# A routed expert layer on one core: token rows gathered by table products instead of through DRAM

## The reference

```python
comb = (p_grp[:, None, None] * grp_1h[:, :, None] * within[:, None, :]).astype(t.dtype)
out = jnp.zeros_like(t)
for gidx in range(N_GROUPS):
    e0 = gidx * EXPERTS_PER_GROUP
    e1 = e0 + EXPERTS_PER_GROUP
    a = jnp.einsum('td,edf->tef', t, w_exp_gate[e0:e1])
    u = jnp.einsum('td,edf->tef', t, w_exp_up[e0:e1])
    act = jax.nn.silu(a) * u * comb[:, gidx, :, None]
    out = out + jnp.einsum('tef,efd->td', act, w_exp_down[e0:e1])
```

## Time and profile before

| | |
|---|---|
| median of 3 runs | 769.56 us (767.94 to 770.43) |
| the profiled execution | 768.86 us, of which the span in the trace is 767.0 |
| PE busy | 713.2 us, 93% of the span |
| DMA moved | 187.25 MB, mean 244 GB/s |
| DVE, ACT, POOL busy | 274.3, 164.1, 61.1 us |
| granted clock of PE, mean | 0.974 |

### The profile page before, as it was taken

The page is one execution under the profiler, slowest core; times in us unless marked ns, Lnnn a source line. Parts: engine busy times, 40 slices in busy tenths (PEclk is TensorE's granted clock), DMA queues, the critical chain, the costliest instruction groups (busy, mean ns, idle before and its releaser), DMA issues.

```text
span 767.0 us, 10734 instructions
## 1 busy us (share of the span) xinstructions
PE 713.2 (93%) x4452; PEld 416.7 (54%) x4452; DVE 274.3 (36%) x733; ACT 164.1 (21%) x377; POOL 61.1 (8%) x91
## 2 busy tenths in 40 slices
PE   7999999999999999999999999999998977878974
PEld 3544557777656877777777775543333322323321
DVE  1241022575865651473264352151222101100335
ACT  3221221322455211321132102231000000000013
POOL 3010200010330000000010020020000000000110
PEclk9999999999999999999999999999999898999997
DMA  9983700770499521043144569487999999999991
GB/s 267 336 299 110 206 15 1 242 283 38 126 394 359 166 68 44 1 144 119 69 131 158 196 223 370 190 330 263 421 427 422 409 432 430 407 427 397 433 347 65
DMA packets 49465, 187.25 MB, mean 244 GB/s; under 512 B 5234, under 2 KB 5479, under 8 KB 45316
## 3 DMA queue, kind: packets, MB, share of 16 engines
q1 hardware_dynamic: 40064, 155.52, 52.4%
q0 software_dynamic: 9200, 30.80, 12.1%
q10 hardware_dynamic: 148, 0.20, 0.1%
HBM read 174.43 MB, written 16.83 MB: 249 GB/s over the span
## 4 chain that ended last, share of the span: by engine, by line
PE 76%; DMA 15%; DVE 4%; issue 2%; ACT 1%; SPq 1%; POOL 1%; DVEq 0%; ACTq 0%
PE PS L669 13%; PE PS L1017 13%; DMA arena<-in_w_exp_down 9%; PE PS L1434 8%; PE PS L1029 6%; PE PS L1468 6%; PE PS L764 5%; DMA ring<-in_w_exp_down 4%; DMA arena<-in_cache_mem_k 2%; PE PS L791 2%; PE PS L680 2%; PE PS L655 2%; PE PS L1316 2%; PE PS L750 1%; PE PS L1116 1%
## 5 line engine op out<-in xcount | busy, mean ns | idle before, releaser
L1434 PE MATMUL PS<-ring,arena 128*64 128x512 f32 x416 | 99.0, 632 | 13.6 <-issue 13.5
L1017 PE MATMUL PS<-hT,ring 128*128 128x288 f32 x384 | 102.2, 414 | 0.0
L1781 ACT ACTIVATE arena<-PS 128x512 f32<-128x512 f32 (+7 forms) x128 | 51.0, 421 | 181.5 <-PE PS L669 50.3
L1017 PEld LDWEIGHTS PS<-hT,ring 128*128 128x128 f32 x384 | 70.1, 190 | 19.6 <-issue 1.5
L1434 PEld LDWEIGHTS PS<-ring,arena 128*64 128x64 f32 x416 | 34.1, 145 | 73.5 <-issue 73.5
L669 PE MATMUL PS<-ring,hT 128*128 128x512 f32 x160 | 70.3, 596 | 0.0
L1781 ACT ACTIVATE brT<-PS 128x256 f32<-128x256 f32 (+4 forms) x37 | 15.6, 424 | 196.7 <-PE PS L1434 153.1
L764 PE MATMUL PS<-hT,ring 128*128 128x288 f32 x192 | 51.2, 422 | 1.3 <-DVE small L2347 1.3
L1029 PE MATMUL PS<-brT,ring 128*128 128x288 f32 x192 | 50.5, 412 | 0.3 <-DVE arena L2581 0.3
L669 PEld LDWEIGHTS PS<-ring,hT 128*128 128x128 f32 x160 | 29.9, 190 | 37.3 <-issue 37.3
L2993 DVE SCALAR_TENSOR_TENSOR brT<-brT,PS 128x256 f32<-128x256 f32 x16 | 6.7, 421 | 111.4 <-ACT brT L1781 111.4
(11 more groups left out here) (394 smaller groups left out, 851.7 us busy)
## 6 DMA issues: line engine op xcount, KB each, us to landing
ring<-in_w_in SPq DMA_DIRECT2D x15, 2048.0 KB, 13.8
ring<-in_w_exp_gate SPq DMA_DIRECT2D x13, 2048.0 KB, 23.9
ring<-in_w_exp_up SPq DMA_DIRECT2D x13, 2048.0 KB, 25.6
ring<-in_w_exp_down SPq DMA_DIRECT2D x8, 2048.0 KB, 24.5
arena<-in_w_exp_down SPq DMA_DIRECT2D x4, 2048.0 KB, 31.5
arena<-in_w_exp_gate SPq DMA_DIRECT2D x3, 2048.0 KB, 17.6
arena<-in_w_exp_up SPq DMA_DIRECT2D x3, 2048.0 KB, 22.5
moe_in<-in_table SPq DMA_DIRECT2D x2, 2048.0 KB, 24.4
```

What stands on the lines that cost most here:

```text
L1017: ins = pe.matmul(PS[:, b, 0:T], w[:, 512 * k + 128 * (c % 4):512 * k + 128 * (c % 4) + 128], hT[:, k, :], start=(k == 0), stop=(k == KD - 1))
L1434: ins = pe.matmul(o[64 * hf:64 * hf + 64, :], hg[:, k, 64 * e:64 * e + 64], w[:, :, 512 * k + 256 * hf:512 * k + 256 * hf + 256], start=(k ...
L1781: return act.activation(o, i, f, **kw)
```

## The change

The rows of all groups are now put into slots by one kind of product. `pick_slots` multiplies a 128-column piece of `h2p` (stationary) by the table of the pair (moving, 128 slots wide), summed over the three token tiles, so that the product comes out already turned, in the PSUM bank that the transposes wrote before. That is 24 matmuls for a pair, 8 pairs in all. The tables of group g+1 are made by DVE after the first expert of group g. `moe_in`, its zeroing, the scatter, the row reads, and ACT's copies of the picked rows are gone. `h2p` stays in place through the stage. Two small things move as well: `tails` gets another place, and `slots_out(1, p, 0)` on DVE stands behind the second expert.

```diff
-        def pick_rows(pr_):
+        def pick_slots(pr_, p, g):
 
-            pe.wait_ge(sg("h2p"), 3)
-            pe.wait_ge(sg("pick"), pr_ + 1)
+            if g == 0 and isinstance(p, int):
+                pe.wait_ge(sg("h2p"), 3)
+            pe.wait_ge(sg("pick"), 2 * G * p + (2 * g + pr_ + 1))
             for hf in range(2):
-                for t, (t0, n) in enumerate(TILES):
-                    ins = pe.matmul(bank_of(("pick", pr_, hf)), pick[pr_][0:n, t, :],
-                                    h2p[0:n, t, 512 * hf:512 * hf + 512], start=(t == 0), stop=(t == 2))
-                ins.then_inc(full[uses[("pick", pr_, hf)][0]], 1)
-
-        def turn_slots(pr_, p, g):
-
-            picked = g == 0 and isinstance(p, int)
-            if not picked:
-                pe.wait_ge(*((sg(f"xg{pr_}"), 16 * (3 * p + g)) if g else (sg(f"xf{pr_}"), 16 * p)))
-            for hf in range(2):
-                if picked:
-                    pe.wait_ge(*taken(("pick", pr_, hf)))
                 pe.wait_ge(*gtaken("xT", 2 * pr_ + hf, p, g))
                 o = gbank("xT", 2 * pr_ + hf)
                 for c in range(4):
-                    ins = pe.transpose(o[:, 128 * c:128 * c + 128],
-                                       xg[pr_][:, 512 * hf + 128 * c:512 * hf + 128 * c + 128], ident)
+                    for t, (t0, n) in enumerate(TILES):
+                        ins = pe.matmul(o[:, 128 * c:128 * c + 128],
+                                        h2p[0:n, t, 512 * hf + 128 * c:512 * hf + 128 * c + 128],
+                                        pick[g][pr_][0:n, t, :], start=(t == 0), stop=(t == 2))
                 ins.then_inc(gfull("xT", 2 * pr_ + hf), 1)
...
-            if g == 0 and isinstance(p, int):
-                pick_rows(0)
             if g == 0:
-                turn_slots(0, p, 0)
+                pick_slots(0, p, 0)
             for e in range(EG):
                 gate_up(e, p, g)
-                if e == 0 and g == 0 and isinstance(p, int):
-                    pick_rows(1)
                 if e == 1 and g == 0:
-                    turn_slots(1, p, 0)
-                if e == 1 and g < G - 1:
-                    turn_slots(0, p, g + 1)
+                    pick_slots(1, p, 0)
+                if e == 1:
+                    pick_slots(0, p, g + 1)
                 if e == 2:
                     turn_act(0, p, g)
                     turn_act(1, p, g)
-                if e == 3 and g < G - 1:
-                    turn_slots(1, p, g + 1)
+                if e == 3:
+                    pick_slots(1, p, g + 1)
...
-            if q == NPAIR - 1:
-                sp.wait_ge(sg("x_out"), 96 * (p + 1))
-                for pr_ in range(FIRST_PAIRS if first else 0, 2):
-                    sp.dma_start(xg[pr_], pair_rows(xrows, pr_, 0)).then_inc(sg(f"xf{pr_}"), 16)
...
-            if unit_no["gout"] <= n < unit_no["gout"] + 2:
-                r = 512 * (n - unit_no["gout"])
-                sp.dma_start(xrows[r:r + 512, :].rearrange("(p c) n -> p c n", p=128), bc(zrow, 128, 4, D)) \
-                    .then_inc(sg("zeroed"), 16)
...
+        def pick_tables(g):
+
+            for pr_ in range(2):
+                e = EG * g + 2 * pr_
+                tt(pick[g][pr_].rearrange("p t (e j) -> p t e j", e=2),
+                   bc(cst[:, C_IOTA:C_IOTA + SLOTS].unsqueeze(1).unsqueeze(1), 128, 3, 2, SLOTS),
+                   bc(rkm[:, :, e:e + 2].unsqueeze(3), 128, 3, 2, SLOTS), ALU.is_equal) \
+                    .then_inc(sg("pick"), 1)
...
-                if e == 0 and g == 0:
+                if e == 0 and g < G - 1:
+                    if g == 0 and isinstance(p, int):
+                        dve.wait_ge(sg("tail_out"), 32)
+                    pick_tables(g + 1)
+                if e == 1 and g == 0:
                     slots_out(1, p, 0)
```

More of the change, by code:

```diff
@@ L77 @@
 C_RST = C_N
-C_Z = C_RST + T
-C_ALL = C_Z + D
+C_ALL = C_RST + T
 NONE = 4096.0
-PASS_STEPS, POOL_TICKS = 15, 16
+PASS_STEPS, POOL_TICKS = 15, 9
 def constants():
@@ L292, in build @@
     qwm, _ = place(M0 + NB * DA, 128, H, NB, NS)
-    tails, _ = place(M0, HIST * (NB + 1), CCH)
+    tails, _ = place(UNIT, HIST * (NB + 1), CCH)
+    assert UNIT + CCH <= B0
     mixed, p = place(B0, 128, KD, T)
@@ L383, in build @@
     ea = route[:, 256:768].rearrange("p (a b) -> p a b", a=2)
-    FIRST_PAIRS = 2
-    pick = [route[:, 768:768 + 6 * SLOTS].rearrange("p (t n) -> p t n", t=3),
-            place(UNIT + D, 128, 3, 2 * SLOTS)[0]][0:FIRST_PAIRS]
+    by_tile = lambda x: x.rearrange("p (t n) -> p t n", t=3)
+    PICK = 6 * SLOTS
+    pick = [[by_tile(route[:, 768:768 + PICK]), by_tile(outp[1][:, 0:PICK])]]
+    pick += [[by_tile(xg[j][:, PICK * pr_:PICK * pr_ + PICK]) for pr_ in range(2)] for j in (0, 1, 0)]
     LG = tiny(128, 3, 20)
@@ L396, in build @@
     msk = tiny(128, 3, E)
-    not_in = tiny(128, 3, EG)[:, :, 0:2 * FIRST_PAIRS]
-    first_rank = tiny(128, 3, EG)[:, :, 0:2 * FIRST_PAIRS]
     rkm = tiny(128, 3, E)
     le4 = tiny(128, 3, E)
+    not_in = le4
+    last_rank = rkm[:, :, E - EG:E]
     wr = tiny(128, KD, 20)
@@ L1707, in waited @@
                 ticks[0] += 1
[L1709 to L1714, removed]
         def gather_rows(p):
@@ L1729, in gather_rows @@
                         .then_inc(sg("rows_in"), 16)
-        def read_slots(pr_, p, g):
-            waited(p)
-            pool.dma_start(xg[pr_], pair_rows(xrows, pr_, g)).then_inc(sg(f"xg{pr_}"), 16)
         def slots_group(p, g):
[L1736 to L1744, removed]
             if g == G - 1:
@@ L2125, in _ @@
         act.preload_act_table_set("exp_and_others")
-        def picked_out(pr_):
-            for hf in range(2):
-                copy_out(("pick", pr_, hf), xg[pr_][:, 512 * hf:512 * hf + 512], bank_of(("pick", pr_, hf)))
-        picked_out(0)
         def group(p, g):
@@ L2875, in pass_weights @@
             step(stt(w_low, slot0, float((E - EG) * SLOTS), w_in_pass, ALU.is_lt, ALU.mult))
-        dstep(dve.memset(first_rank, 0.0))
-        dstep(ts(not_in, msk[:, :, 0:2 * FIRST_PAIRS], 0.0, NONE, ALU.is_equal, ALU.mult))
+        dstep(ts(not_in, msk, 0.0, NONE, ALU.is_equal, ALU.mult))
+        def pick_tables(g):
[5 more added lines that the diff above has]
+                    .then_inc(sg("pick"), 1)
         dve.wait_ge(*filled("rank"))
         for t, (t0, n) in enumerate(TILES):
-            ins = tt(first_rank[0:n, t, :], bank_of("rank")[0:n, E * t:E * t + 2 * FIRST_PAIRS], not_in[0:n, t, :], ALU.add)
+            ins = tt(rkm[0:n, t, :], bank_of("rank")[0:n, E * t:E * t + E], not_in[0:n, t, :], ALU.add)
         dstep(ins)
-        for pr_ in range(FIRST_PAIRS):
-            tt(pick[pr_].rearrange("p t (e j) -> p t e j", e=2),
-               bc(cst[:, C_IOTA:C_IOTA + SLOTS].unsqueeze(1).unsqueeze(1), 128, 3, 2, SLOTS),
-               bc(first_rank[:, :, 2 * pr_:2 * pr_ + 2].unsqueeze(3), 128, 3, 2, SLOTS), ALU.is_equal) \
-                .then_inc(sg("pick"), 1)
-        for t, (t0, n) in enumerate(TILES):
-            ins = cp(rkm[0:n, t, :], bank_of("rank")[0:n, E * t:E * t + E])
-        dstep(ins)
+        pick_tables(0)
         dstep(tt(prod, bc(rkm.unsqueeze(2), 128, 3, 2, E), sel, ALU.mult))
@@ L2915, in last_choices @@
             dstep(tt(last_cmb, lp[:, :, 0, :], lp[:, :, 1, :], ALU.add))
-            dstep(ts(last_rank, msk[:, :, E - EG:E], 0.0, NONE, ALU.is_equal, ALU.mult))
-            dstep(tt(last_rank, last_rank, rkm[:, :, E - EG:E], ALU.add))
         def last_weights():
@@ L3054, in _ @@
                 pass_step(ts(rank2, rank2, -float(SLOTS), None, ALU.add))
-                pass_step(ts(last_rank, last_rank, -float(SLOTS), None, ALU.add))
+                pass_step(ts(rkm, rkm, -float(SLOTS), None, ALU.add))
+                pick_tables(0)
                 slot_ids(p, pass_step)
```

15 lines of the change are left out of this document (removed).

## The result

| | before | changed |
|---|---|---|
| median | 768.75 us (4 runs, 766.83 to 770.43) | 784.87 us (4 runs, 779.13 to 786.95) |
| profiled execution | 768.86 us, span 767.0 | 784.97 us, span 783.1 |
| PE busy | 713.2 us | 752.4 us |
| DMA moved | 187.25 MB | 177.59 MB |
| granted clock of PE, mean | 0.974 | 0.981 |

What follows compares the result with a forecast made beforehand. PE sets the pace at first, the weight stream from about 590 us; with the change PE bounds throughout. Span 714.0 + 8 x 8.35 = 780.8, less 0.2, plus 1.9 outside the span: 782.5 us, range 774 to 789.

Steps and rivals of the forecast that it cites:

- The price of a pick, 8.35: PE's 24 matmuls for a pair: 48 passes give 5.4 us, eight triples add 0.37 us each for changing rows.
- Rival (1): Picks on PE: shape switches cost nothing, 5.4 us a pair, the stream sets the end, 763.5 us, faster; chance 0.09.
- Rival (2): Picks on PE: switches as cheap as in the transposes, 6.6 us a pair, 768.7 us, no change; chance 0.04.
- P: PE's time in us for the pick of one pair, eight pairs in all; taken as 8.35, bounds 5.4 to 9.4.
- PE's sum, 714.0 + 8P: Profiled span if PE never waits for weights: 507.24 + 169.2 + 21.7 + 15.9 us, plus eight picks; 780.8.
- PE doesn't wait for weights: Expert stage: last weights land near 750 us, PE wants them at 757.6; no wait on weights over 1 us.
- 10 us later: First group on PE: the third expert starts 10 us later than in the kernel before.
- DMA share under 0.9 between 535 and 580: Sign of being right: the weight stream's DMA share falls below 0.9 from 535 to 580 us.
- Removed bytes, -5.2 - 0.2: Row reads and later restart in a stream-bound kernel give -5.2 us; zero fills in the branches give -0.2.
- rival (3): PE's clock falls in the picks, 1.7 us a pair, 14 in all, time 796 us; chance 0.07.
- A clock near 0.5 inside picks: Sign of being wrong: PE's granted clock near 0.5 in picks, where 1.0 was expected from 507 to 765 us.

Runs made afterwards that it cites:

- e1_pad: Changed kernel with the sample tile's stationary operand padded with zeros to 128 rows, so the row count never changes in a pick; 762.84 us, 0.9952 of the kernel before.
- e2_outer: Changed kernel with the token-tile loop outside the column loop, so the shape changes once each way in a bank; 766.41 us, 0.9988 of the kernel before.
- e5_apart: Changed kernel with the first group's pick for pair 0 of group 1 moved behind the third expert; 777.63 us, 1.015 of the kernel before.
- e12_adjacent: Changed kernel with the pick for pair 0 of group 1 moved directly ahead of that for pair 1, no wait between; 778.32 us, 1.0122 of the kernel before.

## Why the prediction was right

- **The price of a pick, 8.35.** Measured 8.44: passes of 0.1156 where I had 0.112 (5.55 and not 5.4) and eight triples of 0.36 where I had 0.37. Rival (1) had the right time for a pick without the change of shape, and e1_pad shows what it would have been: 762.84 us, where it gave 763.5. Rival (2) stood for 6.6 and no change; e2_outer, at 6.13 to 6.17, landed at 0.9988, which fits. It does not test the point at which it decides, P = 6.6, as PE still waits for weights in it (1.24, 0.45, 1.60 and 1.36 us late in the run).
- **PE's sum, 714.0 + 8P.** Without the clock fall the stage should have taken 780.6 - 507.24 = 273.4 us. e5_apart, plus the 0.9 of bank wait that it lacks, took 272.0. The sum was 1.4 too long: picks +0.7, the 24 product groups -0.7 (7.02 and not 7.05), the rest, -1.4, is what is left by subtraction, small work between them.
- **PE doesn't wait for weights.** Right, none. The second expert started 15.3 us behind the first pick, 5.2 earlier than before, as forecast; the third 15.8 us later, of which 6.4 is the clock: 9.4 against "10 us later".
- **The stream.** DMA share under 0.9 between 535 and 580: it was 0.53, and 0.68 in e5_apart, without the clock fall. Right.
- **Removed bytes, -5.2 - 0.2.** Measured alone 5.7. In the changed kernel they can have bought next to nothing, as the forecast had it, since PE never waits for weights there; no run takes this apart.
- **The clock, rival (3).** This step failed. I wrote that the branches keep the full clock with small products between large ones, "so I give it little", and priced a fall at 1.7 us a pick. It fell once, at one place, for 17 us: 7.7 us, in both profiles of the kernel. "A clock near 0.5 inside picks" was one of my signs of being wrong, and it came. I had looked at the picks one by one and not at the place where two of them meet with a wait between.
- **What hid that.** The first pick of the profiled execution started at 503.35, not at 507.24 as before: 3.9 us that the sum could not know. Most of it isn't the change: the control of the same kernel started at 506.44, and over all profiles the start lies between 503.2 and 507.2. The kernel before has one profile only, and its start is the latest of all, so a small gain from the missing zero fills can't be ruled out. So the forecast's 782.5 against 784.97 is -3.9 for the start, +7.7 for the clock, -1.4 for the sum. That it came so close is luck, two misses that cancel in part. The direction and the range don't rest on it: without the clock fall the kernel is at 778 (e5_apart, e12_adjacent), 4 to 5 under the forecast, inside the range, and still slower.

The direction rested on the one comparison of line 1316 with line 669 in the trace, and this was what e1_pad and e2_outer confirmed.

## What to carry over

Before replacing transfers by products, price the product by a row with the same sequence of shapes, not only the same size: here alternating 128 and 32 rows turned 5.55 us into 8.44, and padding the short tile with zeros cost nothing and took it back. When a stream of weights has to keep running, look at each place from which it is fed: moving 5.6 us of PE's work within the group in which the stream starts moved the hole, taking work out of that group alone left it, and both together closed most of it (763.32, 763.66 and 757.52 us). And before taking traffic away ask what the replacement does to the engine that is nearly the bound: the bytes alone were worth 5.7 us, and the first version of the replacement put 47 us of work on PE (8 x 8.44 less the 20.5 that went), of which 16 showed in the time.

## What the hardware showed that I had not expected

- Changing the number of active rows between products of 128 columns cost 0.36 us for 128 to 32 and back (8.44 against 5.55 us for eight of these), although a weight load takes nearly the same at either height: by the groups, 186 ns a load of 32 rows and 191 of 128 in e2_outer. The Trainium skill ("TensorE: Matmul & The Clock Gate", LDWEIGHTS) says that a load's time goes by its columns; this agrees, and the cost of the change comes on top of it.
- The granted clock fell to 0.51 (the level of 1.2 GHz) for 17 us though PE was idle only 0.88 us ahead of it and busy all through, in the profiles of the changed kernel and of its control; the same picks in one piece of 16.95 us kept 1.00, and padded picks with the same 0.88 us wait kept it too. Why it falls stays open.
